# Two transformer blocks on one core: the queue place of M5's loads, and three steps of work moved by one or two pieces

## The reference, cut to what matters

```python
merged = sigmoid(g_a) * (y_a @ w_up_a) + sigmoid(g_b) * (y_b @ w_up_b)
x = x + merged @ w_o
hid = rmsnorm(x, ffn_norm_g) @ w_ffn_in
x = x + (silu(hid[:, :F]) * hid[:, F:]) @ w_ffn_out
```

## Time and profile before

| what | us |
|---|---|
| median of 3 runs | 1894.41 (1892.97 to 1895.27) |
| the profiled execution's own time | 1893.05 |
| its span, first to last instruction | 1891.3 |
| TensorE busy in the span | 1877.2 (99%) |
| VectorE busy | 1471.8 (78%) |
| ScalarE busy | 1140.8 (60%) |
| DMA, mean rate | 283 GB/s |

### The profile page before, as it was taken

One profiled execution on the slowest core, in us unless ns is written; L12 is line 12 of the kernel. 1 busy time (PEld: TensorE's weight loads), 2 busy tenths in 40 slices (PEclk: granted clock), 3 DMA queues, 4 the chain that ended last, 5 costly groups with the idle time before them and its releaser, 6 DMA issues.

```text
span 1891.3 us, 23371 instructions
## 1 busy us (share of the span) xinstructions
PE 1877.2 (99%) x9018; PEld 1641.9 (87%) x9018; DVE 1471.8 (78%) x1591; ACT 1140.8 (60%) x1417; POOL 130.4 (7%) x156
## 2 busy tenths in 40 slices
PE   9999999999999999999999999999999999999998
PEld 8888888888888888888888888888888888888887
DVE  6889776655666677778888657988998999898865
ACT  7556445555566556566766455666766676666553
POOL 4000011000001100000000000000000000000000
PEclk9999999999999999999999999999999999999999
DMA  9799898999989879998797886788878887987653
GB/s 392 267 284 310 274 309 272 330 347 327 309 290 312 271 269 299 321 315 278 295 313 247 330 256 239 254 311 284 276 254 320 280 271 257 327 260 249 219 188 130
DMA packets 86815, 535.95 MB, mean 283 GB/s; under 512 B 10416, under 2 KB 11184, under 8 KB 40752
## 3 DMA queue, kind: packets, MB, share of 16 engines
q1 hardware_dynamic: 72736, 458.69, 63.3%
q0 software_dynamic: 13824, 75.50, 20.6%
q10 hardware_dynamic: 144, 0.26, 0.0%
HBM read 529.69 MB, written 105.38 MB: 336 GB/s over the span
## 4 chain that ended last, share of the span: by engine, by line
PE 90%; DVE 5%; DMA 3%; issue 1%; ACT 1%; POOL 0%; SPq 0%; ACTq 0%; DVEq 0%; POOLq 0%
PE acc L1359 44%; PE acc L1364 22%; PE aux L1724 12%; PE aux L1728 6%; DVE wlo L2556 2%; PE aux L1338 2%; DMA ple<-in_w_ffn_in 1%; DVE wlo L1876 1%; PE aux L1431 1%; DVE ple L2551 1%; DMA ple<-in_w_in 1%; DMA raw<-summed 1%; PE aux L1805 0%; ACT whi L928 0%; ACT whi L1177 0%
## 5 line engine op out<-in xcount | busy, mean ns | idle before, releaser
L1876 DVE TENSOR_TENSOR wlo<-raw,whi 128x1024 fp32r<-128x1024 f32 x512 | 623.8, 1226 | 296.4 <-ACT whi L928 288.4
L928 ACT ACTIVATE whi<-raw 128x1024 fp32r<-128x1024 f32 x511 | 534.0, 1054 | 449.8 <-PE acc L1364 414.1
L1359 PE MATMUL acc<-whi,actA_hi 128*128 128x512 f32 x892 | 344.0, 386 | 0.7 <-ACT whi L928 0.7
L1359 PE MATMUL acc<-whi,actA_lo 128*128 128x512 f32 x892 | 339.1, 380 | 0.0
L1359 PE MATMUL acc<-whi,actB_hi 128*128 128x512 f32 x796 | 304.5, 383 | 0.2 <-DVE actB_lo L2673 0.2
L1359 PE MATMUL acc<-whi,actB_lo 128*128 128x512 f32 x796 | 301.7, 379 | 0.0
L1177 ACT ACTIVATE whi<-ple 128x1024 fp32r<-128x1024 f32 x192 | 201.0, 1055 | 139.4 <-PE acc L1364 55.6
L2556 DVE TENSOR_TENSOR wlo<-ple,whi 128x1024 fp32r<-128x1024 f32 x192 | 230.2, 1220 | 31.3 <-ACT whi L1177 28.5
L1364 PE MATMUL acc<-wlo,actA_hi 128*128 128x512 f32 x892 | 229.1, 379 | 0.0
L1364 PE MATMUL acc<-wlo,actB_hi 128*128 128x512 f32 x796 | 204.4, 379 | 0.0
L2556 DVE TENSOR_TENSOR wlo<-raw,whi 128x1024 fp32r<-128x1024 f32 x144 | 174.2, 1220 | 30.6 <-ACT whi L1177 28.9
(11 more groups left out here) (366 smaller groups left out, 2377.0 us busy)
## 6 DMA issues: line engine op xcount, KB each, us to landing
raw<-in_w_in SPq DMA_DIRECT2D x108, 1024.0 KB, 7.3
raw<-in_w_ffn_out SPq DMA_DIRECT2D x44, 1024.0 KB, 6.9
summed<-in_w_ffn_in POOLq DMA_DIRECT2D x36, 1024.0 KB, 11.6
raw<-in_w_ffn_in SPq DMA_DIRECT2D x72, 512.0 KB, 7.9
ple<-summed SPq DMA_DIRECT2D x24, 1024.0 KB, 4.9
raw<-summed SPq DMA_DIRECT2D x48, 512.0 KB, 5.4
ple<-in_w_ffn_in SPq DMA_DIRECT2D x18, 1024.0 KB, 6.9
ple<-in_w_ffn_in POOLq DMA_DIRECT2D x36, 512.0 KB, 9.9
```

What stands on the lines that cost most here:

```text
L928: act.activation(whi[:, g % RING], raw_piece(g), ACT.Copy).then_inc(hi_ready, 1)
L1359: pe.matmul(acc2(n)[:, t, :], act[x][:, k + c, t * P:(t + 1) * P], woven(whi, g, c), start=(p == 0 and c == 0 and x == 0), stop=False)
L1876: dve.tensor_tensor(wlo[:, g % RING], raw_piece(g), whi[:, g % RING].bitcast(F32), ALU.subtract)\
```

## The change

Four edits. (1) M5's loads get a later `free`: the pieces M2 q = 1 and q = 3 in place of M1's. After sorting, the order in a group is: pair, M7 q = 0, M7 q = 1, fifth h = 0, M7 q = 2, M7 q = 3, fifth h = 1, pair, b22. (2) `ml_cols` keeps the transposes; the broadcast is a function of its own, called for i = 0 in the same place and for i = 1 behind piece (11, 0). (3) The scaling stands at w = L0 + 31. (4) The product for ("uB", 2) stands at g = 400 in place of 398.

```diff
-                self.loads.append((self.s_at[c, "M1", 2 * h + 1], self.s_at[c, "M5", 2 * h], "fifth", h, c))
+                self.loads.append((self.s_at[c, "M2", 2 * h + 1], self.s_at[c, "M5", 2 * h], "fifth", h, c))
...
-                for i in range(2):
-                    u = AUX[("bc", i)]
...
+            def ml_rows_spread(i):
+                u = AUX[("bc", i)]
+                free(u)
+                for h in range(2):
+                    ins = pe.matmul(bank(u)[:, h * S:(h + 1) * S], sel[:, 2 * i + h, :], hrow[:, 3, :], start=True, stop=True)
+                ins.then_inc(aux_full, 1)
...
                     if (s, p) == (10, 7):
                         ml_cols()
+                        ml_rows_spread(0)
+                    if (s, p) == (11, 0):
+                        ml_rows_spread(1)
...
-                        if w == L0 + 30:
+                        if w == L0 + 31:
                             powered(dve, f"hB{half}")
...
-                        if g == slab_end(role, j) + (2 if slab_end(role, j) in PLAN.block_end else 3):
+                        last = slab_end(role, j)
+                        if g == last + (2 if last in PLAN.block_end else 5 if (role, j) == ("uB", 2) else 3):
                             u_product(role, j)
```

## The result

The changed kernel takes **1913.31 us** (median of 4 runs, 1910.53 to 1916.99), the kernel before 1894.16 us beside it (4 runs, 1892.97 to 1895.27). The ratio is 1.0102, its 95% interval 1.0082 to 1.0123: about 19 us slower, above the forecast of 1889.7 us and above the whole range. The profiled execution took 1910.53 us, its span is 1908.8 us.

A forecast was written before the change was run, and what follows sets the result against it. TensorE, busy 99% of the span, was taken as the bound. Terms -1.7 - 0.8 - 0.9 - 1.6 + 1.0 = -4.0 us on 1893.05 gave 1889.05, set at 1889.7 us for the median's offset; range 1887.0 to 1897.5.

The forecast's parts named there:

- the step that failed: Ten later groups: 0.64 MB of the fifth uses spare DMA rate, M7's third quarter 1.1 us late; 1.0 us in all.
- The rival's argument: M7's third quarter in ten groups: no unused time can be filled, so the fifth delays it by its whole length; chance 0.22.
- The 2.1 us: Group of 1314 us: slack between VectorE writing M7's third low part (1330.89) and TensorE reading it (1333.01).
- the first rival: Fifth in front of M7's third quarter: ten groups lose 0.8 us each, b22 late 1.3; 1896 to 1901 us, chance 0.22.
- VectorE's lead: At the sums behind b22: takes part of the worst-case lateness of 1.9 us.
- The slack of 4.0 us: b22's first three quarters land at about 1333.6, first sum starts at 1337.62; 4.1 us of delay leaves it 0.1 late.
- the 1.62 us of the forecast: First group: TensorE needs 6.80 us for four short M7 pieces that take 5.18; earlier quarters cover this, gain 1.6 us.
- mechanism: Decay rows' broadcast: full matmuls between two shorter 4-row stretches keep the clock up; gain 1.7 us, bounds 0 and 1.7.
- brought no fall: In front of L1452: TensorE idle for 2.6 us without a clock fall, so edit 2's shorter stretches should not cause one.
- The second rival: Clock at the broadcast falls all the same, or falls elsewhere: sum -2.3, 1891.4 us, chance 0.17.
- forecast 0.9: Piece 399: moving the gate product to g = 400 removes TensorE's wait; gain 0.9 us, bounds 0 and 0.95.
- The sum: Whole kernel: -1.7 - 0.8 - 0.9 - 1.6 + 1.0 = -4.0 us on the profiled 1893.05.

The follow-up runs named there:

- run 4: All four edits, but both fifths of a group stand behind all four of M7's quarters; against the kernel before: 1901.85 us, 1.0037.
- Run 8: The changed kernel with the residual's addition in groups 5, 8 and 9 two pieces later; against the kernel before: 1907.27 us, 1.0069.
- run 2: Edits 2 to 4 without edit 1, against the kernel before: 1891.85 us, 0.9986.
- run 3: Edits 2 to 4, and edit 1 in the first group only, against the kernel before: 1891.18 us, 0.9990.
- run 1: Edit 1 alone, the other three undone, against the kernel before: 1908.87 us, 1.0071.
- run 5: Edits 2 to 4, and only the second fifth behind M7, against the kernel before, run twice: 1889.70 and 1889.59 us, 0.9972 both times.

## Why the prediction was wrong

**Edit 1, the ten groups: the step that failed.** It said that (358 - 197) x 4 us = 0.64 MB of a fifth "fit into what was unused", so that the third quarter is late by 1.1 us, within 2.1 us of slack, and put 0.1 us on each group. It is late by 3.3 us in that group and by 3.7 us on the mean of the ten. The window at a low rate was not room: with a fifth queued in it the engines carried 238 GB/s in place of 206, and on the mean of the ten groups no more than before. The room was earlier, where the fifths stood, and the change left it empty (0 GB/s in 1321.00:1324.10). The rival's argument, a fifth's whole length in front of the quarter, was the right one; run 4 shows that taking it away takes the 12.2 us away. Its 2.9 us were too few, since they were worked out at 358 GB/s: at the 264 GB/s of this stretch 1.05 MB take 4.0 us by estimate. The Trainium skill, DMA: Bandwidth & Descriptors, section "Two DMAs through the same engine are not ordered", says that within one queue of a DMA engine descriptors start in order. The order of M7's landings agrees with that (5.89, 10.05 and 11.28 us, with the fifth between the first two of these, at 8.83), and it should have had more weight than an average rate. To stand ahead of the fifth is no full protection either: M7's second quarter, issued 0.4 us before it, lands at 5.6 us on the mean of the ten groups, and at 4.0 us in run 4, where the fifths come later.

**The slack was read at one consumer.** Slack is how much later a transfer may land before TensorE waits. The 2.1 us were right for six of the ten groups: by the landing of the third quarter and the loss at M5, a group loses what the landing exceeds 8.8 us by, and 6.76 + 2.1 is 8.9. In the four others VectorE has another job between the third and the fourth low part, a residual addition in groups 5, 8 and 9 and a gate product in group 2, and the limit is 7.8 us or less:

| group | third quarter lands, us from M2 | lost by M5, us | landing minus loss |
|---|---|---|---|
| 1 | 10.17 | 1.45 | 8.7 |
| 3 | 9.54 | 0.73 | 8.8 |
| 4 | 9.66 | 0.86 | 8.8 |
| 6 | 9.46 | 0.65 | 8.8 |
| 10 | 9.52 | 0.79 | 8.7 |
| 7 | 8.01 | 0.00 | |
| 2 | 9.56 | 2.04 | 7.5 |
| 5 | 10.05 | 2.29 | 7.8 |
| 8 | 9.54 | 1.78 | 7.8 |
| 9 | 9.46 | 1.62 | 7.8 |

The group that I read was one of the four, and the earlier trace rows break off at the third low part. The two lines of VectorE behind it in the kernel before, and TensorE's reading of the fourth low part:

```profile
1330.81 1.21 DVE L2718 TENSOR_TENSOR resid<-resid,acc 128x1024 f32<-128x1024 f32 x1
1331.94 1.22 DVE L2556 TENSOR_TENSOR wlo<-raw,whi 128x1024 fp32r<-128x1024 f32 x1
```

```profile
1334.31 0.59 PE L1728 MATMUL aux<-wlo,actB_hi 128*128 128x512 f32 x2
```

From the end of the fourth low part to its reading there are 1.15 us; by the landings (7.8 - 6.76) the slack is 1.0 us. Run 8, which moves that job away, is the test of this. For this reason the first rival's price, 0.8 us a group and 1.3 with b22, was too low as well: the groups lost 2.0 us each in all (20.3 us).

**b22 and what stands behind.** I priced the sums at 0.1 us late, and 1.9 us at the worst with "part of which VectorE's lead takes". The slack of 4.0 us was misread: the first b22 quarter landed at 1334.6 us, not at 1333.6, because the last landed at 1338.4 and the four stand 1.2 to 1.3 us apart, not 1.5; that leaves 3.0 us. Run 4 has the sums alone: b22 is 4.2 us late there, the first sum 1.2 us, and 7.3 us are lost over ten groups. The lead I counted on isn't there in four groups at M6, and not at the end of the group either: M4's additions land just when ScalarE wants them, before and after. In the changed kernel VectorE comes late to M6 by M7's lateness rather than by b22's (b22's first quarter lands at 17.4 us, its sum starts at 19.1 us, with no wait for DMA), and the cost behind M5 is 8.1 us.

**Edit 1, the first group: right.** TensorE there in the changed kernel, with the two rows that answer to the earlier trace rows:

```profile
862.21 1.03 PE L1364 MATMUL acc<-wlo,actB_hi 128*128 128x512 f32 x4
868.25 0.38 PE L1359 MATMUL acc<-whi,actB_hi 128*128 128x512 f32 x1
```

From one to the other it takes 6.04 us in place of 7.66: the 1.62 us of the forecast. The first quarter's wait of 4.64 us is gone. The third quarter lands 1.5 us sooner and not 2.9, which is enough. The further 0.6 us at this group's M4 isn't the edit's: it is there in run 2 too (0.9), and half of it in the second trace of the kernel before (0.35).

**Edit 2: mechanism right, size 1.3 in place of 1.7.** The fall of the clock behind the broadcast is gone in ten traces of ten. The two pieces around it took 4.85 + 4.38 us and take 3.99 + 3.84 us, and the next 0.10 us more. The fall lasts 3.41 us, so it costs 1.71; of these, 0.41 are given back, and the same 4-row work takes that much longer in two parts.

**"One fall" was one execution.** I read from one trace that L1452's wait "brought no fall". It does in 11 of 14, at 1.4 to 1.7 us each by the starts, and the profile of after has it. The wait itself is 2.6 us in all 14. The second rival, that the clock falls elsewhere, describes that trace, but for another reason: the fall doesn't move there, since it comes without the edits too. The Trainium skill, TensorE: Matmul & The Clock Gate, Part 1, says that the window in which the activity is judged runs freely, and that the same kernel therefore shows a different number of slowed matmuls from run to run. 11 of 14 agrees with that, and no run here tests it.

**Edit 3: 0.55 us in place of 0.8.** TensorE's wait before L1431 is gone (1.01 us between two starts), but 0.29 and 0.18 us come back in the pieces behind it, where I had put the scaling in VectorE's idle time at no cost. Over the traces that have the edit it is 0.4 to 0.55 us.

**Edit 4: 0.4 to 1.1 us, forecast 0.9, and nothing in the changed kernel.** In run 3 piece 399 is followed after 1.30 us in place of 2.35. In run 2 ScalarE waits 0.5 us longer for piece 399's load; 0.56 us come out, and 0.41 of them are left behind the product. In the changed kernel the load comes later still: ScalarE's split starts 2.0 us later than before, counted from piece 398. Its wait, 3.41 us in the earlier trace rows:

```profile
1028.59 1.06 ACT L1177 ACTIVATE whi<-ple 128x1024 fp32r<-128x1024 f32 x1 [3.91 <-DMA ple<-in_w_in]
```

There piece 399 is followed after 1.80 us; but it is followed after 1.79 us in run 1 too, where edit 4 is undone. With the load late, VectorE has finished the product before piece 399's high part is there, and its place costs nothing. The split behind the product in run 1:

```profile
1031.75 1.22 DVE L2556 TENSOR_TENSOR wlo<-ple,whi 128x1024 fp32r<-128x1024 f32 x1 [0.33 <-ACT whi L1177]
```

So edit 1 takes edit 4's gain away. The sum, which added the edits up, had no such term.

**The three together** were forecast at 3.4 us and measured at 2.7 us (0.9986; 1.5 us by the medians). The gains of the sum, 5.0 us with the first group's, meet the 5 us of run 5, and this is partly luck: in its traces the four parts are 1.3, 0.5, 0.6 to 0.9 and 1.6 us, 4.0 to 4.3 in all, and the rest is tenths at the ends of groups that no term names. What sank the sum is its one positive term, +1.0 us where the traces have +20.3.

**Open.** Runs of the same order differ: edit 1 alone has a ratio of 1.0071 and all four edits 1.0102, although edits 2 to 4 gain 2.7 us by themselves. Their profiled executions took 1910.10 and 1910.53 us. M7's landings vary by a microsecond between executions, and each counts in full once the slack is gone; whether the order also takes back the three edits' gains was not measured in one comparison. Edit 4's lost gain is a part of it. And why the engines move only 262 to 295 GB/s in the 4.5 us behind M2's start (means of the ten groups in the 14 traces; single groups have 207 to 372), at a share of 0.8 to 0.9, was not tried.

## What to carry to other kernels

A stretch in which DMA runs at a low rate isn't free room: look whether the queue had work in it, and look for a stretch at 0 GB/s, here 3 us that the change itself made. When a transfer is put in front of another in a queue, charge its whole length at the rate of that stretch, not of a full one (1 MB, 2.9 us at 358 GB/s, made the next transfer 3.7 us late), to everything behind it. Follow the lateness through each in-order engine to the last consumer: the slack of a chain is its smallest one, and it differs from group to group with the other jobs in the list. A load whose data are wanted last can go behind those wanted first, as the second fifth does, but it is worth moving only the one that lands in room on both sides. Gains at places that feed each other don't add up, as edit 4's with edit 1. And a feature that a trace shows once, such as a fall of the clock or its absence, wants a second trace before it enters a sum.

## What the runs showed of the hardware

- The granted clock fell to 0.50 (1.2 in place of 2.4 GHz) for about 3.4 us behind 2.2 us of matmuls on 4 rows in 4 of 4 traces, and in 0 of 10 with 2.6 us of full matmuls in the middle. Behind a 2.6 us wait of TensorE it fell in 11 of 14, at a cost of 1.4 to 1.7 us.
- Eight matmuls of 4 rows by 256 columns cost 0.4 us more in two stretches than in one (by the starts around them in 10 traces).
- In the changed kernel the queue moved 238 GB/s in the 4.5 us behind M2's start and 397 GB/s in the 11.4 us behind that (windows 1327.10:1331.60 and 1331.60:1343.00), with transfers outstanding throughout. On the mean of the ten groups it moved 264 GB/s in the first 4.5 us and 366 in the next.
- A transfer of 512 KB was made late by a 1 MB transfer issued 0.4 us behind it in the same queue: it landed at 5.6 us from M2's start in place of 4.0 on the mean of ten groups (changed kernel and run 4).
